# Two of four weight sums of a pair made by adding transfers on GpSimd's queue, with the weight slots turned and the normalisation and splits re-ordered to suit

## The chip, the cores and the metric

The kernel runs on one core of one Trainium2 chip. The metric is the device time of one execution in microseconds; times given are medians of several executions.

## The reference

One layer is computed: an RMS norm, a projection into eight attention heads and a pooling mixer, and an output projection with a second RMS norm and a residual. With a sequence of 512 and a width of 2048:

```python
hn = _rmsnorm(h, pre_norm_gain[layer])
proj = jnp.einsum('bsd,de->bse', hn, w_in[layer])        # 2048 -> 6 * 1024
q, k, v, g_a, u_b, g_b = jnp.split(proj, split_at, axis=-1)
y_a = _stick_breaking(heads(q), heads(k), heads(v))       # 8 heads of 128
y_a = y_a.transpose(0, 2, 1, 3).reshape(b, s, D_SB) * jax.nn.silu(g_a)
y_b = _multiscale_pool(u_b, w_pool[layer], pool_scale[layer]) * jax.nn.silu(g_b)
mix = jnp.concatenate([y_a, y_b], axis=-1)
out = jnp.einsum('bse,ed->bsd', mix, w_out[layer])
h = h + _rmsnorm(out, post_norm_gain[layer])
```

All of it is float32.

## The kernel before, in words

**Split operands.** TensorE multiplies in a rounded format, so each float32 operand is split in two: ScalarE copies it to a rounded high part (`w_hi`, `x_hi`, `a_hi`), VectorE subtracts to get the rest (`raw_lo`, `x_lo`, `a_lo`), and three matmuls (`three`, L1232 to L1234) make one product. `raw_lo` lies on the same bytes as `raw`, so a slot of `raw` is taken from the landing of its weights until the TensorE step that uses it is done. There are 7 such slots of 512 KB.

**Stage 1, the values.** `values_step(i)`, 16 steps, multiplies raw tokens times gain (`xT`, tiles of `mix`) by the value weights. In the same time the kernel prepares the left operands of everything that follows. ScalarE squares the token rows (`square_of`, L471, 128x2048 each), VectorE makes the mean square (`ms_col`), GpSimd raises it to -0.5 (L1205), and its queue stores this to DRAM (`rstd_dram`) and loads it back spread over all partitions (`rstd_rows`). `hn_of(q)` then normalises four tiles of `mix` in place (L847), and for each of four groups q seven operands of a Strassen product are made and split: A11, R1, S2, S4, S3, A12, A22. These have the counters `a_summed`, `a_hi_done` and `a_split`. Group q is spread over the iterations i = 4 + 3q, 5 + 3q and 6 + 3q of the loops of ScalarE and VectorE. In iteration i these engines also split x of step i + 3 and the weights of step i + 2. `v_drain` copies the finished values out of PSUM, scaled by `rstd_col`.

**Stage 2, the pairs (the body).** 20 units u of 7 products each (Strassen-Winograd: 7 products of 128x1024 weights in place of 8). Product p of unit u is `step_of(u, p)`, 24 matmuls. Its weights are four parts of two chunks (p = 0, 4, 3, 5, loaded by `load_b`) and four sums of them (p = 1, 2, 6, 4), made by VectorE in `w_sum` (L827). Between the products lie the score, suffix-sum, value and pooling matmuls of the heads; GpSimd masks (`mask`, L1216). The order of the work is written out by hand per unit kind r and product p. `ROLE[u][p]` is the slot of a product's weights: a permutation carried from unit to unit.

**Stage 3, the output projection.** `rows_tile` multiplies the split `mix` (`mix_hi_of`, `mix_lo_of` at L1032) by the split output weights (`o_hi_of` at L655, `o_lo_of` at L1041); squares, norm, residual and store follow.

**Queues.** All loads are on SyncE's queue. A load waits there for the step that frees its slot: before, (0, 4, 3, 5) of the next unit wait for steps 0, 1, 2, 3 of this one.

Of the kernel before, what the change touches and what calls it, by code (L numbers as in the profile page):

```python
# [5 lines left out]
F32 = mybir.dt.float32  # L6
# [77 lines left out]
def slot_turns():  # L84
# [10 lines left out]
    for u in range(UNITS):  # L95
        for p in (0, 4, 3, 5):
            lands((u, p), ROLE[u][p])
# [8 lines left out]
def hybrid_layer(nc, xT, x, pre_gain, w_v, w_heads, w_pool, pool_scale, w_out, post_gain, out):  # L106
    with ExitStack() as ctx:
# [27 lines left out]
        rstd_col = sb("rstd_col", [P, TT])  # L135
        ss_col = sb("ss_col", [P, TT])
# [88 lines left out]
        w_summed = sem("w_summed")  # L225
        step_done = sem("step_done")
# [6 lines left out]
        rstd_spread = sem("rstd_spread")  # L233
        hn_done = sem("hn_done")
# [108 lines left out]
        def _(sp):  # L343
# [26 lines left out]
            load_x_rows(0)  # L370
            load_x(4)
            load_v(4)
            load_x_rows(1)
            load_x_rows(2)
            load_x(5)
            load_v(5)
            load_x_rows(3)
            load_x(6)
            load_v(6)
            sp.dma_start(pool_scale_col[:, :], pool_scale).then_inc(scale_loaded, 16)  # L380
            for i in range(7, V_STEPS):
                load_x(i)
                load_v(i)
                if i == 15:
                    pass

            def load_b(u, p):
                n1, n2 = unit_chunks(u)
                n = n1 if p in (0, 5) else n2
# [8 lines left out]
            for p, last in ((0, 9), (4, 10), (3, 11), (5, 12)):  # L398
                sp.wait_ge(step_done, last + 1)
                load_b(0, p)  # L400
            for u in range(LAST_UNIT):
# [4 lines left out]
                for p, freed in ((0, 0), (4, 1), (3, 2), (5, 3)):  # L406
                    sp.wait_ge(step_done, step_of(u, freed) + 1)
                    if r == 3 and p == 5:
# [33 lines left out]
        def _(act):  # L442
# [11 lines left out]
            def w_hi_of(g):  # L454
# [5 lines left out]
                elif p in (0, 3, 5):  # L460
                    act.wait_ge(raw_loaded[slot], TURN[u, p])
                else:
                    act.wait_ge(w_summed, 4 * u + (1, 2, 6, 4).index(p) + 1)
# [22 lines left out]
            def a_hi_raw(q):  # L486
                act.wait_ge(hn_done, 4 * (q + 1))
                for op, half, tok in ((A11, 0, 0), (A12, 1, 0), (A22, 1, 1)):
                    act.activation(split3(operand(a_hi, op, q)), pairs(mix, q, half, tok),  # L489
                                   ACT.Copy).then_inc(a_hi_done, 1)  # L490

            def a_hi_sum(q, op):
                act.wait_ge(a_summed, 4 * q + (R1, S2, S3, S4).index(op) + 1)
                dst = operand(a_hi, op, q)
                if op == R1:
                    act.activation(dst, sum1[:, :], ACT.Copy).then_inc(a_hi_done, 1)
                elif op == S2:
                    act.activation(dst, sum2[:, :], ACT.Copy).then_inc(a_hi_done, 1)
                elif op == S3:
                    act.activation(split3(dst), pairs(mix, q, 0, 1), ACT.Copy).then_inc(a_hi_done, 1)  # L500
                else:
                    act.activation(split3(dst), pairs(mix, q, 1, 0), ACT.Copy).then_inc(a_hi_done, 1)
# [19 lines left out]
            x_hi_of(1)  # L522
            w_hi_of(1)
            x_hi_of(2)
            for i in range(V_STEPS):
                if i + 3 < V_STEPS:
                    x_hi_of(i + 3)
                w_hi_of(i + 2)
                if i == 1:
                    square_of(0)  # L530
                if i == 2:
                    square_of(1)
                    square_of(2)
                if i == 3:
                    square_of(3)
                q, part = (i - 4) // 3, (i - 4) % 3
                if i >= 4:
                    if part == 0:
                        a_hi_raw(q)
                        a_hi_sum(q, R1)  # L540
                    if part == 1:
                        a_hi_sum(q, S2)
                        a_hi_sum(q, S3)
                    if part == 2:
                        a_hi_sum(q, S4)
            act.wait_ge(rstd_ready, 1)
            v_drain(0, 0)
            v_drain(0, 1)
# [921 lines left out]
```

## Time and profile before

| what | value |
|---|---|
| median of 3 runs | 778.89 us (775.41 to 779.28) |
| the profiled execution | 779.01 us, span 777.3 us |
| mean granted TensorE clock | 0.98 |
| TensorE busy | 740.6 us of the span (95%) |
| VectorE, ScalarE busy | 525.5 us (68%), 389.8 us (50%) |
| stages | values to about 113 us, body from 119 to 584 us, output to the end |

The span runs from the first to the last instruction; the profiled execution took 1.7 us more than that. Busy shares are means over three stages that differ, so the stages are read apart. The granted clock is full at 1.00; 0.50 is the lower level.

### The profile page before, as it was taken

How to read it: one execution, taken by the hardware profiler on the slowest of the kernel's cores; microseconds unless marked ns; L12 is line 12 of the kernel's file. 1: busy time of each engine (PE TensorE's matmuls, PEld its weight loads, DVE VectorE, ACT ScalarE, POOL GpSimd, SP SyncE). 2: the span in 40 equal slices, each digit the busy share in tenths (PEclk: the TensorE clock that was granted, in tenths of full speed). 3: DMA queues.
4: the chain of work that ended last, by engine and by line, in shares of the span. 5: the costliest groups of instructions: out<-in, count | busy, mean ns of one | idle time of the engine just before them, and what ended most of it. 6: DMA issues, size and time to landing. Idle time of an engine off the chain costs nothing.

```text
span 777.3 us, 11793 instructions
## 1 busy us (share of the span) xinstructions
PE 740.6 (95%) x4912; PEld 685.2 (88%) x4912; DVE 525.5 (68%) x612; ACT 389.8 (50%) x530; POOL 29.8 (4%) x47
## 2 busy tenths in 40 slices
PE   7938988999999999999999999999997999999996
PEld 5827868999999999999999999999996888888885
DVE  4318896797977897877897977897867713142233
ACT  4615546655566655566655566655577522132200
POOL 0100000010000010010010010010000000000000
PEclk9977998999999999999999999999999999999999
DMA  8942203222233222233222233212245504142232
GB/s 322 381 108 63 87 28 108 82 74 98 91 109 109 79 73 98 92 110 109 78 72 98 94 109 109 77 71 98 96 147 206 183 35 162 55 149 78 99 136 108
DMA packets 27716, 87.02 MB, mean 112 GB/s; under 512 B 3152, under 2 KB 4176, under 8 KB 27024
## 3 DMA queue, kind: packets, MB, share of 16 engines
q1 hardware_dynamic: 27408, 86.00, 31.7%
q8 instruction: 39, 0.64, 0.3%
q0 software_dynamic: 112, 0.26, 0.2%
q14 instruction: 13, 0.11, 0.0%
q10 hardware_dynamic: 144, 0.01, 0.0%
HBM read 82.06 MB, written 4.20 MB: 111 GB/s over the span
## 4 chain that ended last, share of the span: by engine, by line
PE 83%; DVE 8%; ACT 3%; DMA 3%; issue 2%; POOL 0%; DVEq 0%; POOLq 0%; SPq 0%; ACTq 0%
PE ps L1232 27%; PE ps L1233 26%; PE ps L1234 26%; DVE raw_lo L802 2%; PE ps L1323 1%; PE ps L1321 1%; DVE mix L847 1%; DMA rstd_dram<-rstd_col 1%; DMA rstd_rows<-rstd_dram 1%; DVE a_lo L862 1%; ACT w_hi L466 1%; ACT a_hi L489 1%; PE ps L1249 0%; DVE a_lo L879 0%; DMA raw<-w_v 0%
## 5 line engine op out<-in xcount | busy, mean ns | idle before, releaser
L1232 PE MATMUL ps<-a_hi,w_hi 128*128 128x256 f32 x1120 | 319.8, 286 | 5.9 <-ACT mix L513 5.9
L1233 PE MATMUL ps<-a_lo,w_hi 128*128 128x256 f32 x1120 | 318.6, 284 | 0.0
L1234 PE MATMUL ps<-a_hi,raw_lo 128*128 128x256 f32 x1120 | 318.6, 284 | 0.0
L1232 PEld LDWEIGHTS ps<-a_hi,w_hi 128*128 128x128 f32 x1120 | 215.6, 192 | 6.6 <-issue 6.3
L1233 PEld LDWEIGHTS ps<-a_lo,w_hi 128*128 128x128 f32 x1120 | 215.5, 192 | 0.3
L1234 PEld LDWEIGHTS ps<-a_hi,raw_lo 128*128 128x128 f32 x1120 | 215.4, 192 | 0.0
L802 DVE TENSOR_TENSOR raw_lo<-raw,w_hi 128x1024 fp32r<-128x1024 f32 x155 | 189.6, 1223 | 37.9 <-ACT w_hi L466 37.3
L466 ACT ACTIVATE w_hi<-raw 128x1024 fp32r<-128x1024 f32 x155 | 163.5, 1055 | 75.2 <-PE ps L1234 73.0
L827 DVE TENSOR_TENSOR raw<-raw 128x1024 f32<-128x1024 f32 x80 | 98.7, 1234 | 1.5 <-PE ps L1234 1.5
L1232 PE MATMUL ps<-a_hi 128*128 128x512 f32 x192 | 75.5, 393 | 3.9 <-DVE a_lo L1032 3.9
L1234 PE MATMUL ps<-a_hi,a_lo 128*128 128x512 f32 x192 | 75.5, 393 | 0.0
L1233 PE MATMUL ps<-a_lo,a_hi 128*128 128x512 f32 x192 | 75.4, 393 | 0.0
L1232 PE MATMUL ps<-w_hi,x_hi 128*128 128x512 f32 x120 | 48.4, 403 | 14.4 <-DVE raw_lo L802 14.4
L1041 DVE TENSOR_TENSOR a_lo<-raw,a_hi 128x1024 fp32r<-128x1024 f32 x24 | 28.3, 1222 | 42.3 <-ACT a_hi L655 42.3
L1233 PE MATMUL ps<-raw_lo,x_hi 128*128 128x512 f32 x120 | 48.5, 404 | 0.0
L1234 PE MATMUL ps<-w_hi,x_lo 128*128 128x512 f32 x120 | 48.4, 404 | 0.0
L1232 PEld LDWEIGHTS ps<-a_hi 128*128 128x128 f32 x192 | 36.3, 189 | 11.8 <-issue 4.1
L655 ACT ACTIVATE a_hi<-raw 128x1024 fp32r<-128x1024 f32 x24 | 24.0, 1049 | 44.6 <-PE ps L1234 44.6
L1216 POOL TENSOR_SCALAR_AFFINE_SELECT tri<-tri 128x256 f32<-128x256 f32 x32 | 24.1, 775 | 527.4 <-DVE tri L951 429.0
L1234 PEld LDWEIGHTS ps<-a_hi,a_lo 128*128 128x128 f32 x192 | 36.4, 189 | 7.6
L1233 PEld LDWEIGHTS ps<-a_lo,a_hi 128*128 128x128 f32 x192 | 36.3, 189 | 7.6
L1232 PEld LDWEIGHTS ps<-w_hi,x_hi 128*128 128x128 f32 x120 | 23.3, 194 | 20.2 <-issue 14.8
(140 smaller groups left out, 849.4 us busy)
## 6 DMA issues: line engine op xcount, KB each, us to landing
raw<-w_heads SPq DMA_DIRECT2D x80, 512.0 KB, 3.5
raw<-w_out SPq DMA_DIRECT2D x32, 512.0 KB, 4.8
raw<-w_v SPq DMA_DIRECT2D x15, 512.0 KB, 10.0
mix<-xT SPq DMA_DIRECT2D x16, 256.0 KB, 9.9
x_rows<-x SPq DMA_DIRECT2D x4, 1024.0 KB, 13.6
raw<-x SPq DMA_DIRECT2D x8, 512.0 KB, 4.4
out<-mix SPq DMA_DIRECT2D x6, 512.0 KB, 2.7
wp_raw<-w_pool SPq DMA_DIRECT2D x8, 128.0 KB, 2.1
```

The source lines that it names most:

```text
L466: act.activation(hi_slot(g), raw_slot(raw, slot), ACT.Copy).then_inc(w_hi_done, 1)
L489: act.activation(split3(operand(a_hi, op, q)), pairs(mix, q, half, tok), ACT.Copy).then_inc(a_hi_done, 1)
L655: act.activation(out_weights(a_hi, o_hi3, n % OUT_SLOTS)[:, b * QUARTER:(b + 1) * QUARTER], raw_slot(raw, half_slot(j)), ACT.Copy).then_in ...
L802: dve.tensor_tensor(raw_slot(raw_lo, slot), raw_slot(raw, slot), hi_slot(g).bitcast(F32), ALU.subtract).then_inc(w_split, 1)
L827: dve.tensor_tensor(raw_slot(raw, ROLE[u][p]), raw_slot(raw, ROLE[u][a]), raw_slot(raw, ROLE[u][b]), ALU.add).then_inc(w_summed, 1)
L847: dve.scalar_tensor_tensor(mix_tile(k), mix_tile(k), pre_gain_col[:, k:k + 1], rstd_rows[:, :], ALU.mult, ALU.mult).then_inc(hn_done, 1)
L862: dve.tensor_tensor(split3(operand(a_lo, op, q)), pairs(mix, q, half, tok), split3(operand(a_hi, op, q)).bitcast(F32), ALU.subtract).then_ ...
L1041: dve.tensor_tensor(out_weights(a_lo, o_lo3, n % OUT_SLOTS)[:, cols], raw_slot(raw, half_slot(j)), out_weights(a_hi, o_hi3, n % OUT_SLOTS) ...
L1216: pool.affine_select(out=sq, in_=sq, compare_op=ALU.is_gt, fill=0.0, base=0, pattern=[[0, 2], [1, P]], channel_multiplier=-1).then_inc(don ...
L1232: pe.matmul(dst, sta[0], mov[0], start=first, stop=False, skip_group_check=True)
L1233: pe.matmul(dst, sta[0], mov[1], start=False, stop=False, skip_group_check=True)
L1234: return pe.matmul(dst, sta[1], mov[0], start=False, stop=last, skip_group_check=True)
```

## The change

Five edits come together.

1. `t1` (p = 1, was 0 + 4) and `t3` (p = 4, was a part of its own with 4 + 3) are no longer VectorE sums. SyncE loads one part plainly into the slot of p = 1 and of p = 4; GpSimd's queue then issues a transfer of 512 KB that adds the other part to it in SBUF (`add_b`). In this split of the work p = 1 takes the first part of both chunks, and p = 4 the two second parts. VectorE keeps p = 2 and p = 6. ScalarE waits for the new counters `t1_summed` and `t3_summed`.
2. `ROLE` and the order of loads follow: five plain loads per unit, (1, 0, 4, 3, 5), waiting for steps 0 to 4.
3. The token rows are loaded earlier, in a layout with four consecutive tokens on a partition; the squares follow at once; the reciprocal root is stored and spread by ScalarE's queue, the store in runs of 16 bytes. A third small transfer brings `rstd_col`.
4. The order of splitting the operands is turned to A11, R1, S2, S4, S3, A12, A22, the order of the products, and S3, A12, A22 of the last group are split in the first products of the body. The first product waits for A11 alone.
5. In the last unit the splits of `mix` tiles 0 to 3 come at products 1 to 3, and the first output weights are split ahead of the softplus.

```diff
-ROLE = [[2, 6, 0, 4, 3, 5, 1]]
+ROLE = [[3, 2, 0, 5, 4, 6, 1]]
-    ROLE.append([_r[0], _r[4], _r[5], _r[2], _r[1], _r[3], _r[6]])
+    ROLE.append([_r[1], _r[0], _r[5], _r[3], _r[2], _r[4], _r[6]])
...
+            by_four = x.rearrange("t (q s) d -> (t q) s d", s=TT)
-                sp.dma_start(x_rows[:, s * D:(s + 1) * D], x[s]).then_inc(x_rows_loaded[s], 16)
+                sp.dma_start(x_rows[:, s * D:(s + 1) * D], by_four[:, s, :]).then_inc(x_rows_loaded[s], 16)
...
-            for p, last in ((0, 9), (4, 10), (3, 11), (5, 12)):
+            for p, last in ((1, 9), (0, 10), (4, 11), (3, 12), (5, 13)):
...
-                for p, freed in ((0, 0), (4, 1), (3, 2), (5, 3)):
+                for p, freed in ((1, 0), (0, 1), (4, 2), (3, 3), (5, 4)):
...
+                elif p == 1:
+                    act.wait_ge(t1_summed, 16 * (u + 1))
+                elif p == 4:
+                    act.wait_ge(t3_summed, 16 * (u + 1))
...
+                if i == 3:
+                    act.wait_ge(rstd_ready, 1)
+                    act.dma_start(rstd_dram.rearrange("(p s) -> p s", s=TT),
+                                  rstd_by_four[:, :]).then_inc(rstd_sent, 16)
...
+                if i == 3:
+                    act.wait_ge(rstd_sent, 16)
+                    act.dma_start(rstd_rows[:, :],
+                                  rstd_dram.partition_broadcast(P)).then_inc(rstd_spread, 16)
+                    act.dma_start(rstd_col[:, :], rstd_dram.rearrange("(s p) -> p s", p=P),
+                                  allow_slow_non_contiguous=True).then_inc(rstd_col_loaded, 16)
...
                     if last:
                         if p == 1:
                             mix_hi_of(0)
-                        if p == 4:
-                            for k in (1, 2, 3):
-                                mix_hi_of(k)
-                        if p == 5:
-                            o_hi_of(0)
+                            mix_hi_of(1)
+                        if p == 2:
+                            mix_hi_of(2)
+                            mix_hi_of(3)
...
+            def a_sum4(q):
+                dve.wait_ge(a_split, PRODUCTS * q + R1 + 1)
+                dve.wait_ge(a_summed, 4 * q + 2)
+                dve.scalar_tensor_tensor(split3(sum1[:, :]), pairs(mix, q, 1, 0), -1.0,
...
-                    if p == 1:
-                        w_sum(u, 4)
-                    if p in (5, 6) and not last:
-                        w_sum(u + 1, p - 4)
+                    if p == 6 and not last:
+                        w_sum(u + 1, 2)
+                    if u == 0 and p < 3:
+                        a_lo_of(3, (S3, A12, A22)[p])
...
+            def add_b(u, p, done):
+                slot = ROLE[u][p]
+                a = 0 if p == 1 else QUARTER
+                pool.wait_ge(raw_loaded[slot], TURN[u, p])
+                if u:
+                    pool.wait_ge(w_hi_done, step_of(u - 1, p) + 1)
+                pool.dma_start(raw_slot(raw, slot), w_heads[unit_chunks(u)[1]][:, a:a + QUARTER],
+                               accum_op=ALU.add).then_inc(done, 16)
+            add_b(0, 1, t1_summed)
+            add_b(0, 4, t3_summed)
+            for u in range(UNITS):
...
+                if r in (0, 2) and u:
+                    h = h0 - 1 if r == 0 else h0
+                    pool.wait_ge(weights_exp, h + 1)
+                    mask(weights_masked)
+                if u < LAST_UNIT:
+                    add_b(u + 1, 1, t1_summed)
+                if r in (1, 4):
+                    pool.wait_ge(softplus_done, h0 + 1 if r == 1 else h0 + 2)
+                    mask(softplus_masked)
+                if u < LAST_UNIT:
+                    add_b(u + 1, 4, t3_summed)
...
-                    pe.wait_ge(a_split, PRODUCTS * 3 + (1, 4, 5, 7, 7, 7, 7)[p])
+                    pe.wait_ge(a_split, PRODUCTS * 3 + p + 1)
```

ScalarE in the values stage, the kernel before, from the split of x of step 4 on (L451 splits x, L466 the weights, L471 squares token rows, L489 is the first operand copy):

```order
L451 ACTIVATE x_hi0<-mix,pre_gain_col 128x512 [waits step_done,x_loaded4]
L466 ACTIVATE w_hi<-raw 128x1024 [waits step_done,raw_loaded3]
L471 ACTIVATE x_rows,ss_col<-x_rows 128x2048 [waits x_rows_loaded0]
L451 ACTIVATE x_hi1<-mix,pre_gain_col 128x512 [waits step_done,x_loaded5]
L466 ACTIVATE w_hi<-raw 128x1024 [waits step_done,raw_loaded4]
L471 ACTIVATE x_rows,ss_col<-x_rows 128x2048 [waits x_rows_loaded1]
L471 ACTIVATE x_rows,ss_col<-x_rows 128x2048 [waits x_rows_loaded2]
L451 ACTIVATE x_hi2<-mix,pre_gain_col 128x512 [waits step_done,x_loaded6]
L466 ACTIVATE w_hi<-raw 128x1024 [waits step_done,raw_loaded5]
L471 ACTIVATE x_rows,ss_col<-x_rows 128x2048 [waits x_rows_loaded3]
```

The same place now (L470 splits weights, L475 squares):

```order
L475 ACTIVATE x_rows,ss_col<-x_rows 128x2048 [waits x_rows_loaded2]
L475 ACTIVATE x_rows,ss_col<-x_rows 128x2048 [waits x_rows_loaded3]
L451 ACTIVATE x_hi0<-mix,pre_gain_col 128x512 [waits step_done,x_loaded4]
L470 ACTIVATE w_hi<-raw 128x1024 [waits step_done,raw_loaded4]
L451 ACTIVATE x_hi1<-mix,pre_gain_col 128x512 [waits step_done,x_loaded5]
L533 DMA rstd_dram<-rstd_by_four 128x4 [waits rstd_ready]
L451 ACTIVATE x_hi2<-mix,pre_gain_col 128x512 [waits step_done,x_loaded6]
L470 ACTIVATE w_hi<-raw 128x1024 [waits step_done,raw_loaded5]
L541 DMA rstd_rows<-rstd_dram 128x512 [waits rstd_sent]
L543 DMA rstd_col<-rstd_dram 128x4x1
L451 ACTIVATE x_hi3<-mix,pre_gain_col 128x512 [waits step_done,x_loaded7]
L470 ACTIVATE w_hi<-raw 128x1024 [waits step_done,raw_loaded6]
```

All four squares now stand ahead of the split of step 4, and ScalarE's own queue waits for the store to land before it goes on to x of step 7 and the weights of step 6.

GpSimd, from the reciprocal root into the first units, before:

```order
L1205 TENSOR_TENSOR rstd_col<-ms_col,neg_half 128x4 [waits vec_const,ms_ready]
L1208 DMA rstd_dram<-rstd_col 128x4x1 [waits rstd_ready]
L1211 DMA rstd_rows<-rstd_dram 128x512 [waits rstd_sent]
L1216 AFFINE_SELECT tri<-tri 128x2x128 [waits softplus_done]
L1216 AFFINE_SELECT tri<-tri 128x256
```

and now (L1228 is the adding transfer, L1218 the mask):

```order
L1212 TENSOR_TENSOR rstd_by_four<-ms_col,neg_half 128x4 [waits vec_const,ms_ready]
L1228 DMA raw<-w_heads 128x1024 [waits raw_loaded2]
L1228 DMA raw<-w_heads 128x1024 [waits raw_loaded4]
L1228 DMA raw<-w_heads 128x1024 [waits w_hi_done,raw_loaded3]
L1228 DMA raw<-w_heads 128x1024 [waits w_hi_done,raw_loaded0]
L1228 DMA raw<-w_heads 128x1024 [waits w_hi_done,raw_loaded2]
L1218 AFFINE_SELECT tri<-tri 128x2x128 [waits softplus_done]
L1218 AFFINE_SELECT tri<-tri 128x256
```

Forty adding transfers stand between the sixteen pairs of masks, two for each unit.

ScalarE at the end of the last unit, before (L643 splits `mix` tiles, L590 the softplus, L655 output weights):

```order
L466 ACTIVATE w_hi<-raw 128x1024 [waits step_done,w_summed]
L643 ACTIVATE a_hi<-mix 128x512 [waits y_free,step_done] x3
L590 ACTIVATE tri_hi<-tri 128x1280 [waits pool_done,softplus_masked]
L655 ACTIVATE a_hi<-raw 128x1024 [waits raw_loaded2,step_done]
L655 ACTIVATE a_hi<-raw 128x1024 [waits raw_loaded3]
```

and now (L470, L665 and L600 are the same operations):

```order
L470 ACTIVATE w_hi<-raw 128x1024 [waits step_done,w_summed]
L665 ACTIVATE a_hi<-raw 128x1024 [waits raw_loaded2,step_done]
L665 ACTIVATE a_hi<-raw 128x1024 [waits raw_loaded3]
L600 ACTIVATE tri_hi<-tri 128x1280 [waits pool_done,softplus_masked]
```

The three `mix` tiles have gone to earlier products, and the output weights no longer stand behind the masked softplus.

## Rows read from the trace of the kernel before

**Rows 1.** The page, part 1: busy us, share of the span, instructions.

```profile
PE 740.6 (95%) x4912; PEld 685.2 (88%) x4912; DVE 525.5 (68%) x612; ACT 389.8 (50%) x530; POOL 29.8 (4%) x47
```

**Rows 2.** Waits of TensorE: us in total, times, longest.

```profile
PE ps L1232 <- DVE raw_lo L802: 14.4, 1, 14.4
...
PE ps L1232 <- DVE a_lo L1032: 3.9, 1, 3.9
```

**Rows 3.** Timeline of TensorE: start us, us, instruction, idle time before it.

```profile
12.64 0.40 PE L1232 MATMUL ps<-w_hi,x_hi 128*128 128x512 f32 x1
...
46.01 0.39 PE L1234 MATMUL ps<-w_hi,x_lo 128*128 128x512 f32 x1
60.80 0.76 PE L1232 MATMUL ps<-w_hi,x_hi 128*128 128x512 f32 x1 [14.40 <-DVE raw_lo L802]
...
67.17 0.39 PE L1232 MATMUL ps<-w_hi,x_hi 128*128 128x512 f32 x1
...
112.94 0.40 PE L1234 MATMUL ps<-w_hi,x_lo 128*128 128x512 f32 x1
...
119.20 0.55 PE L1232 MATMUL ps<-a_hi,w_hi 128*128 128x256 f32 x1 [5.87 <-ACT mix L513]
...
125.05 0.28 PE L1232 MATMUL ps<-a_hi,w_hi 128*128 128x256 f32 x1
...
588.03 0.48 PE L1232 MATMUL ps<-a_hi 128*128 128x512 f32 x1 [3.91 <-DVE a_lo L1032]
```

**Rows 4.** TensorE by stretch: length, busy (matmuls), granted clock, DMA share, GB/s.

```profile
64.00:66.00 2.00, 2.00 (x6) 0.50 0.00 0
...
122.00:125.00 3.00, 3.00 (x16) 0.50 0.00 0
...
590.00:592.00 2.00, 2.00 (x6) 0.50 1.02 354
```

**Rows 5.** The chain that ended last, 0 to 180 us: start, us, what.

```profile
31.34 2.00 ACT x_rows L471 x2
...
34.93 10.12 DMA rstd_dram<-rstd_col
...
45.35 7.50 DMA rstd_rows<-rstd_dram
```

**Rows 6.** Timeline of ScalarE, the split of x of step 5.

```profile
24.41 0.72 ACT L451 ACTIVATE x_hi<-mix,pre_gain_col 128x512 fp32r<-128x512 f32 x1 [3.37 <-DMA mix<-xT]
```

**Rows 7.** DMA issues: count, KB each, median us from issue to landing.

```profile
raw<-w_heads SPq DMA_DIRECT2D x80, 512.0 KB, 3.5
...
rstd_rows<-rstd_dram POOLq DMA_DIRECT2D x1, 256.0 KB, 7.5
pre_gain_col<-pre_gain ACTq DMA_DIRECT2D x1, 8.0 KB, 3.0
```

**Rows 8.** Timeline of VectorE in the values stage, groups 1 to 3.

```profile
70.19 2.73 DVE L847 SCALAR_TENSOR_TENSOR mix<-mix,pre_gain_col,rstd_rows 128x512 f32<-128x512 f32 x4
...
75.79 0.75 DVE L794 SCALAR_TENSOR_TENSOR x_lo<-mix,pre_gain_col,x_hi 128x512 fp32r<-128x512 f32 x1 [2.15 <-ACT x_hi L451]
...
104.16 2.74 DVE L847 SCALAR_TENSOR_TENSOR mix<-mix,pre_gain_col,rstd_rows 128x512 f32<-128x512 f32 x4
```

**Rows 9.** All engines by stretch, the body (PE, PEld, DVE, ACT, POOL busy).

```profile
130.00:580.00 450.00, 450.00 (x3630) 445.37 (x3629) 369.81 (x407) 271.91 (x359) 23.35 (x30) 1.00 0.27 96
```

**Rows 10.** Timeline of ScalarE in one unit (r = 3).

```profile
308.64 0.38 ACT L557 ACTIVATE q_raw<-ps 128x256 f32<-128x256 f32 x1 [1.55 <-PE ps L1234]
...
324.48 1.06 ACT L466 ACTIVATE w_hi<-raw 128x1024 fp32r<-128x1024 f32 x1 [0.78 <-PE ps L1234]
...
330.18 0.39 ACT L557 ACTIVATE mix<-ps 128x256 f32<-128x256 f32 x1 [1.03 <-PE ps L1234]
```

**Rows 11.** Timelines at the end of the last unit: ScalarE, then VectorE.

```profile
579.77 1.27 ACT L590 ACTIVATE tri_hi<-tri 128x1280 fp32r<-128x1280 f32 x1 [2.95 <-POOL tri L1216]
...
582.03 2.36 DVE L1041 TENSOR_TENSOR a_lo<-raw,a_hi 128x1024 fp32r<-128x1024 f32 x2 [2.58 <-ACT a_hi L655]
```

More of the change, by code:

```diff
@@ L95, in slot_turns @@
     for u in range(UNITS):
-        for p in (0, 4, 3, 5):
+        for p in (1, 0, 4, 3, 5):
             lands((u, p), ROLE[u][p])
@@ L369, in _ @@
                 load_v(i)
[L370 to L376, printed above, removed]
+                load_x_rows(i - 1)
             load_x_rows(3)
-            load_x(6)
-            load_v(6)
+            for i in (4, 5, 6):
+                load_x(i)
+                load_v(i)
             sp.dma_start(pool_scale_col[:, :], pool_scale).then_inc(scale_loaded, 16)
@@ L726, in _ @@
                         if p == 5:
+                            if last:
+                                o_hi_of(0)
                             softplus_hi_of(h1)
@@ L859, in a_lo_raw @@
                 dve.tensor_tensor(a21, pairs(mix, q, 0, 0), a21, ALU.subtract).then_inc(a_summed, 1)
-                for n, (op, half, tok) in enumerate(((A11, 0, 0), (A12, 1, 0), (A22, 1, 1))):
-                    dve.wait_ge(a_hi_done, PRODUCTS * q + n + 1)
-                    dve.tensor_tensor(split3(operand(a_lo, op, q)), pairs(mix, q, half, tok),
-                                      split3(operand(a_hi, op, q)).bitcast(F32),
-                                      ALU.subtract).then_inc(a_split, 1)
@@ new lines, in a_lo_of @@
+            def a_lo_of(q, op):
+                dve.wait_ge(a_hi_done, PRODUCTS * q + op + 1)
+                hi, lo = operand(a_hi, op, q).bitcast(F32), operand(a_lo, op, q)
+                if op in (A11, A12, A22, S3):
+                    half, tok = {A11: (0, 0), A12: (1, 0), A22: (1, 1), S3: (0, 1)}[op]
+                    dve.tensor_tensor(split3(lo), pairs(mix, q, half, tok), split3(hi),
+                                      ALU.subtract).then_inc(a_split, 1)
+                else:
+                    dve.tensor_tensor(lo, (sum2 if op == S2 else sum1)[:, :], hi,
@@ L915, in _ @@
                         hn_of(q)
+                        a_lo_of(q, A11)
                     if part == 1:
-                        a_lo_raw(q)
+                        a_sums(q)
+                        a_lo_of(q, R1)
+                        a_lo_of(q, S2)
                     if part == 2:
-                        a_lo_sums(q)
+                        a_sum4(q)
+                        a_lo_of(q, S4)
+                        if i < V_STEPS - 1:
+                            for op in (S3, A12, A22):
+                                a_lo_of(q, op)
             def combine(u, p):
```

170 lines of the change are left out of this document (71 added, 99 removed).

## The prediction

> **What bounds the kernel now.** I read the shares first: TensorE is busy for 740.6 of 777.3 us [rows 1], so at most 36.7 us of the span can be won without fewer matmuls. Then its waits, which say where these lie. Three stand after the start: 14.4 us for the low part of a weight (VectorE), 5.9 us for a drain of the values (ScalarE), and 3.9 us for a split `mix` tile (VectorE) [rows 2, 3]. Then the body alone: from 130 to 580 us TensorE is busy for 450.00 of 450.00 us at full clock, VectorE for 369.81 and ScalarE for 271.91 [rows 9]. So in the body nothing waits for VectorE, and work taken from VectorE there gives nothing by itself. The reader should see that the change is worth what it does to the two ends of the body, less what its new waits cost inside.
>
> Each gap costs more than its length. After the 14.4 us gap the stretch 64 to 66 us has a granted clock of 0.50, after the 5.9 us gap the stretch 122 to 125 us has it too, and after the 3.9 us gap 590 to 592 us [rows 4]: 1.2 in place of 2.4 GHz, after TensorE had stood still.
>
> The chain tells why the first gap is there. The last square ends at 33.3, the store of the root begins 1.6 us later and takes 10.12 us, the spread 7.50 us, to 52.9 [rows 5]; VectorE, whose order has `hn_of(0)` ahead of the weights of step 7, stands until then, and TensorE, done with step 6 at 46.2, until 60.8 [rows 3].
>
> **Term 1, the values stage.** Steps 1 to 6 ran from 12.64 to 46.24 (46.01 plus one pitch of 0.23), 5.60 us each; later, at full clock, 201 matmuls went from 67.17 to 113.17, a pitch of 0.229 or 5.49 us for a step of 24 [rows 3]. With no wait the stage ends at 12.64 + 6 x 5.60 + 9 x 5.49 = 95.7 us, and the first product starts there, not at 119.2: 23.5 us.
>
> Does it have no wait? (a) The rows. x of step 5 landed at 24.4 [rows 6], behind 7,168 KB in queue order. That is now the place of the last token rows: the last square runs from 24.4 to 26.4, and the root is ready 1.6 us later as before, at 28.0. x and weights of step 4 are 768 KB more; at the mean rate so far (7,168 KB in 24.4 us) that is 2.6 us, so they are there at 27.0, and copy (1.0) and subtraction (1.2) end at 29.2. Step 4 starts at 12.64 + 3 x 5.60 = 29.4. That just fits; half a microsecond lost is possible. (b) The round trip. ScalarE issues the store after the splits of steps 4 and 5, at about 28.7. A store on its queue: the nearest row is the gain's load, 128 rows on the same queue, 3.0 us [rows 7]; the other end is 10.1 us, the old store [rows 5], which had four times as many pieces. I take 3.5. The spread: the old one took 7.5 on GpSimd's queue [rows 5]; the lower end is 3.0, the gain's row. I take 5.0, between. Behind the wait for the store stand x of step 7 and the weights of step 6 (wanted at 40.6), behind the spread `hn_of(0)` and then the weights of step 7 (wanted at 46.2). After the rows land, VectorE and ScalarE need some 6.8 us: normalising 2.7 [rows 8], ScalarE's copies of A11, R1 and x 0.6 to 0.7 each, copy and subtraction of the weights 2.2. Landing by 39.4 costs nothing. 28.7 + 3.5 + 0.4 + 5.0 = 37.6: no wait. Store and spread together may take 10.3 us. (c) The pace. A group of three iterations took (104.16 - 70.19) / 2 = 17.0 us on VectorE, of which 2.15 us was a wait for x_hi behind four operand copies of ScalarE [rows 8]. Now two copies stand ahead of it and one split (0.6 us) lies in the wait: about 1 us of wait left, and 0.7 more for S4: some 16.5 us, against 16.5 that TensorE needs for three steps. It keeps pace. (d) The end. The drain waited for S4, the last sum (ScalarE, before); now it stands ahead of S4, and product 0 wants A11 only. The 5.9 us go; they are within the 23.5.
>
> **Term 2, clock at the start of the body.** From 119.20 to 125.05 the matmuls had a pitch of 0.213; at full clock it is 0.12. 27 matmuls x 0.094 = 2.6 us. Without the gap this is not paid.
>
> **Term 3, the end of the last unit.** VectorE waited 2.58 us for the split of the first output weights, which ScalarE made behind the masked softplus (579.77) [rows 11]; the `mix` tiles followed, and TensorE stood 3.9 us [rows 2]. TensorE had ended product 6 at 588.03 - 3.91 = 584.1 [rows 3]; product 4 was done two products of 2.9 us and 1.4 us of pooling earlier, at about 577. Now the weights are split from then on, 2 us on ScalarE and 1.2 more on VectorE, which is through by 582, and the tiles were made earlier. I take the whole 3.9 and, for 8 matmuls at half the clock [rows 4], pitch 0.43 instead of 0.23, 1.6, less 0.5 for a remainder: 5.0 us.
>
> **Term 4, the body.** VectorE loses 40 sums, SyncE gains 20 loads, GpSimd gains 40 adding transfers. The load of p = 1 of the next unit is issued when product 0 is done (308.64), lands 3.5 us later (312.1) [rows 7, 10]; then the adding transfer starts. ScalarE took up these weights at 324.48, and TensorE wanted them at about 330.1, when product 0 of the next unit was done [rows 10]; copy and subtraction take 2.3 us, so the transfer may take 330.1 - 2.3 - 312.1 = 15.7 us at no cost. For p = 4 the room is no smaller: its load comes two products later and its use three. In units where a mask stands ahead in GpSimd's queue, the mask waits for matmuls that lengthen the unit as much. What does an adding transfer of 512 KB take? No row shows one. Lower end: 3.5 us, the plain load [rows 7]. Upper end: the 256 KB spread on the same software queue, 7.5 us, doubled: 15.0. Being on that queue and reading two streams, I take 10. All three are under 15.7, so the term is 0, hidden behind five products.
>
> The Trainium skill ("DMA: Bandwidth & Descriptors", Anatomy of one DMA) gives 2.0 us plus bytes over 436 GB/s for a transfer of GpSimd's queue. By it 512 KB take 3.2 us and the 256 KB spread 2.6, where the trace has 7.5; the trace decides, and by the page term 4 is 0 as well, with a wider margin.
>
> **Sum.** 779.0 - 23.5 - 2.6 - 5.0 - 0 = 747.9, say 748.0 us. It is made against the profiled execution (779.01), which stands 0.1 us above the median of the runs.
>
> **Rivals.**
> - *The round trip of the root stays slow.* For it: the loads of the values stage still fill the same transfer engines then, and the old store took 10.1 us. With 5.0 and 7.5 us the rows land at 41.6, 2.2 us late: 750 us. With the old 10.1 and 7.5 the rows land at 46.7, and step 7 starts 7.3 us late; the half clock after it took 15 matmuls from 60.80 to 67.17 [rows 3], 15 x (0.425 - 0.229) = 2.9 us: 758.2. Against: a quarter of the pieces, another queue. Chance 0.20.
> - *The hand-over still waits.* ScalarE's drain, or the low parts that follow it, come late in the first unit, as before: 5.9 + 2.6 stay: 756.5. Against: a drain now needs only the first 0.7 us of step 15 and A-operands of groups done long ago. Chance 0.07.
> - *Slower: the adding transfers land too late.* If one takes X us, each of the 19 units that follow another pays X - 15.7, ScalarE's queue standing at the copy of p = 1 and VectorE behind it. The gain of 31.1 is eaten at X = 15.7 + 31.1 / 19 = 17.3. The mechanism that could bring it there: GpSimd writes the pieces of each transfer itself beside a VectorE that is busy for 82% of the body [rows 9]. If it had only VectorE's idle 18% for that, each microsecond of writing would take 5.6: 15.0 + 4.6 = 19.6 for one such microsecond, and 748 + 19 x 3.9 = 822 us. The Trainium skill ("SBUF — State Buffer", Who interferes with whom) says that VectorE's two-port modes lock GpSimd out of writing descriptors, but that tensor_tensor, the form here, is inferred not to. Chance 0.08.
> - *The adds are late in some kinds of unit only,* by 1 to 2 us: 755 to 768. Chance 0.05.
> - *The forecast:* 745 to 750.5. Chance 0.60.
>
> **How the numbers follow.** About 0.5% (4 us) is what a measurement of this kernel can tell from no change. All cases but the third end below 775: faster 0.90, same 0.02 (adds late by 1.5 us), slower 0.08. The range takes in the forecast, the slow round trip and the late hand-over, and about 1 us for the runs' own spread: 744 to 760.
>
> **What would show it.** In the profile after: the first body matmul near 96 us; no TensorE wait over 1 us between 12 and 560; granted clock 1.00 throughout; `hn_of(0)` starting near 38; the first `rows_tile` right behind product 6. The landing time of the adding transfers decides term 4: under 15.7 us it is nothing, and ScalarE's copies of p = 1 stand where they stood. Wrong would be: a wait of TensorE for ScalarE's or VectorE's weights once per unit, or a body longer than 465 - 2.6 us.

## The result and the profile after

The changed kernel takes **754.49 us** (median of 4 runs, 753.12 to 756.16), the kernel before on the same chip 779.09 us (775.41 to 780.76): ratio **0.9691, 95% interval 0.9652 to 0.9731**. The profiled execution took 756.16 us with a span of 754.4; it is the longest of the four.

The page of the changed kernel first, busy time of each engine and, of the 40 slices, TensorE and its granted clock:

```profile
PE 736.1 (98%) x4912; PEld 679.6 (90%) x4912; DVE 481.5 (64%) x572; ACT 389.9 (52%) x530; POOL 62.4 (8%) x85
...
PE   7999989999999999999999999999999999999996
...
PEclk9999999999999999999999999999999999999999
```

TensorE has the same 4,912 matmuls as in [rows 1]; its 4.5 us less of busy time are matmuls that no longer run at half clock. The prediction took the 36.7 us of idle time as the most that can be won without fewer matmuls; that is too little by this part, since matmuls at half clock count as busy. VectorE has 40 instructions and 44 us less, and GpSimd twice its busy time. What won the time is in TensorE's waits (engine, tile, line, releaser: us in total, times, longest), where 14.4, 5.9 and 3.9 us stood before [rows 2, 3]:

```profile
PE ps L1274 <- ACT w_hi L520: 5.3, 1, 5.3
...
PE ps L1257 <- DVE raw_lo L813: 2.4, 2, 1.8
PE ps L1257 <- ACT p_neg L571: 1.3, 1, 1.3
PE ps L1257 <- ACT mix L514: 1.1, 1, 1.1
PE ps L1257 <- ACT work L567: 1.1, 1, 1.1
```

The first is the start of the program and was there before. TensorE's timeline has the places of the others, and the first `rows_tile` matmul, which now has no gap ahead of it:

```profile
49.71 0.47 PE L1257 MATMUL ps<-w_hi,x_hi 128*128 128x512 f32 x1 [1.84 <-DVE raw_lo L813]
...
101.45 0.36 PE L1257 MATMUL ps<-a_hi,w_hi 128*128 128x256 f32 x1 [1.11 <-ACT mix L514]
...
108.53 0.36 PE L1257 MATMUL ps<-a_hi,w_hi 128*128 128x256 f32 x1 [1.09 <-ACT work L567]
...
112.97 0.36 PE L1257 MATMUL ps<-a_hi,w_hi 128*128 128x256 f32 x1 [1.33 <-ACT p_neg L571]
...
566.88 0.40 PE L1257 MATMUL ps<-a_hi 128*128 128x512 f32 x1
```

With 119.20 and 588.03 from [rows 3] these split the 22.9 us between the spans (the medians of the runs are 24.6 us apart, as the profiled execution of the changed kernel is its longest):

| stretch | before | after | difference | predicted |
|---|---|---|---|---|
| to the first product of the body | 119.20 | 101.45 | -17.75 | -23.5 |
| the body, to the end of product 6 | 464.92 | 465.43 | +0.5 | -2.6 |
| from there to the end, gap included | 193.18 | 187.52 | -5.66 | -5.0 |

The first row hangs on the pair of executions. Two runs below have the values stage of the kernel before, but for a sum or two on VectorE; their first product starts at 122.01 and 121.52. Six have the one of the changed kernel, and start it at 99.05 to 101.85. The means (120.9 of three, 100.4 of seven) are 20.5 us apart, not 17.75.

The stretches behind the two hand-overs, and the body (length; PE, PEld, DVE, ACT, POOL busy; granted clock, DMA share, GB/s), answer to [rows 4, 9]:

```profile
102.00:105.00 3.00, 3.00 (x28) 3.00 (x26) 2.30 (x4) 1.18 (x3) 0.00 (x0) 1.00 0.00 0
...
567.00:569.00 2.00, 2.00 (x11) 1.62 (x10) 1.44 (x2) 1.97 (x4) 0.00 (x0) 1.00 0.61 154
...
130.00:560.00 430.00, 430.00 (x3465) 425.31 (x3464) 313.58 (x355) 262.47 (x346) 50.75 (x64) 1.00 0.61 161
```

The clock is full in all three. In the body TensorE is again busy all the time, while VectorE's busy share falls from 82% to 73%: nothing waited for it, so nothing came of that. The DMA issues (KB each, median us to landing) have the adding transfers, and the round trip of the root:

```profile
raw<-w_heads SPq DMA_DIRECT2D x100, 512.0 KB, 4.2
raw<-w_heads POOLq DMA_DIRECT2D x40, 512.0 KB, 6.4
...
rstd_rows<-rstd_dram ACTq DMA_DIRECT2D x1, 256.0 KB, 6.7
rstd_dram<-rstd_by_four ACTq DMA_DIRECT2D x1, 2.0 KB, 6.0
```

ScalarE's timeline in the values stage shows how that trip lies: store issued at 29.84, spread at 35.84, and x of step 7 behind the wait for the store. In the chain, VectorE's first group (`mix` L848) starts at 42.61, the next at 59.34 and 76.07:

```profile
29.84 0.33 ACTq L533 DMA_DIRECT2D rstd_dram<-rstd_by_four  x1
...
35.84 0.33 ACTq L541 DMA_DIRECT2D rstd_rows<-rstd_dram  x1
...
37.03 0.72 ACT L451 ACTIVATE x_hi<-mix,pre_gain_col 128x512 fp32r<-128x512 f32 x1 [3.66 <-PE ps L1259]
```

```profile
29.84 5.97 DMA rstd_dram<-rstd_by_four
35.84 6.75 DMA rstd_rows<-rstd_dram
42.61 2.75 DVE mix L848 x4
...
59.34 2.75 DVE mix L848 x4
...
76.07 2.74 DVE mix L848 x4
```

### The profile page after: what moved, and what is told of

Its sections match the earlier page's. It is cut to its first block, busy times and chain, and to the rows that moved or that the text cites. A ratio compares the mean times of both kernels' runs of the same rounds, so it can differ in the third digit from the quotient of the medians.

```text
span 754.4 us, 11839 instructions
## 1 busy us (share of the span) xinstructions
PE 736.1 (98%) x4912; PEld 679.6 (90%) x4912; DVE 481.5 (64%) x572; ACT 389.9 (52%) x530; POOL 62.4 (8%) x85
## 4 chain that ended last, share of the span: by engine, by line
PE 83%; DVE 7%; DMA 4%; issue 3%; ACT 2%; SPq 1%; DVEq 0%; POOLq 0%; POOL 0%; ACTq 0%
PE ps L1257 27%; PE ps L1258 27%; PE ps L1259 27%; DMA mix<-xT 2%; PE ps L1348 1%; DVE mix L848 1%; DVE raw_lo L813 1%; PE ps L1346 1%; DMA rstd_rows<-rstd_dram 1%; DVE a_lo L881 1%; DVE a_lo L878 1%; DMA rstd_dram<-rstd_by_four 1%; ACT w_hi L470 1%; SPq L367 1%; DVE sum L853 0%
## 5 line engine op out<-in xcount | busy, mean ns | idle before, releaser
L813 DVE TENSOR_TENSOR raw_lo<-raw,w_hi 128x1024 fp32r<-128x1024 f32 x155 | 189.3, 1223 | 58.7 <-ACT w_hi L470 58.0
L470 ACT ACTIVATE w_hi<-raw 128x1024 fp32r<-128x1024 f32 x155 | 163.5, 1055 | 75.7 <-PE ps L1259 71.5
L1228 POOL DMA_DIRECT2D raw<-w_heads x40 | 34.9, 871 | 322.4 <-DMA raw<-w_heads 286.1
L828 DVE TENSOR_TENSOR raw<-raw 128x1024 f32<-128x1024 f32 x40 | 48.8, 1220 | 10.5 <-DMA raw<-w_heads 9.5
L665 ACT ACTIVATE a_hi<-raw 128x1024 fp32r<-128x1024 f32 x24 | 24.1, 1051 | 45.2 <-PE ps L1259 45.2
L1218 POOL TENSOR_SCALAR_AFFINE_SELECT tri<-tri 128x256 f32<-128x256 f32 x32 | 24.0, 772 | 165.3 <-ACT tri L604 84.9
```

The costliest lines, as they stand in the source:

```text
L470: act.activation(hi_slot(g), raw_slot(raw, slot), ACT.Copy).then_inc(w_hi_done, 1)
L665: act.activation(out_weights(a_hi, o_hi3, n % OUT_SLOTS)[:, b * QUARTER:(b + 1) * QUARTER], raw_slot(raw, half_slot(j)), ACT.Copy).then_in ...
L813: dve.tensor_tensor(raw_slot(raw_lo, slot), raw_slot(raw, slot), hi_slot(g).bitcast(F32), ALU.subtract).then_inc(w_split, 1)
L828: dve.tensor_tensor(raw_slot(raw, ROLE[u][p]), raw_slot(raw, ROLE[u][a]), raw_slot(raw, ROLE[u][b]), ALU.add).then_inc(w_summed, 1)
L1218: pool.affine_select(out=sq, in_=sq, compare_op=ALU.is_gt, fill=0.0, base=0, pattern=[[0, 2], [1, P]], channel_multiplier=-1).then_inc(don ...
L1228: pool.dma_start(raw_slot(raw, slot), w_heads[unit_chunks(u)[1]][:, a:a + QUARTER], accum_op=ALU.add).then_inc(done, 16)
```

## The experiments

Four questions: which part of the change wins the time; why the first term came 5.75 us short; how much room the adding transfers have; what the better order would give.

### Which part wins

**The changed kernel without adding transfers.** The values stage and the end as changed; in the body the old sums, slots and loads.

```diff
+                    if p == 1:
+                        w_sum(u, 4)
-                    if p == 6 and not last:
-                        w_sum(u + 1, 2)
+                    if p in (5, 6) and not last:
+                        w_sum(u + 1, p - 4)
...
-            add_b(0, 1, t1_summed)
-            add_b(0, 4, t3_summed)
```

> The changed kernel with the four sums back on VectorE, the old slots and the four plain loads; the new values stage and the new end are kept. Theory A (the adding transfers are hidden and the sums on VectorE were never waited for in the body; the gain is at the two ends): 754 to 758 us, the only cost being one or two sums of 1.2 us on VectorE at the hand-over to the body. Theory B (the adding transfers cost time in the body, by their load on DMA or by late landing): 3 us or more under the changed kernel, 751 us or less. Theory C (the sums taken from VectorE are the gain): 770 us or more.

Measured 755.72 us (755.11 to 758.16), ratio 0.9703 (0.9675 to 0.9731): the changed kernel's time.

**The adding transfers alone,** put into the kernel before with their slots and loads.

> The kernel before with the adding transfers, their slots and loads, and nothing else of the change. Theory A: 776 to 779 us, since the body has no wait to win and only the hand-over has one or two sums less. Theory B: over 779. Theory C: 755 to 765 us.

Measured 780.14 us (777.30 to 781.75), ratio 1.0005 (0.9989 to 1.0021). The time is above the 776 to 779 us expected, but the kernel before took 780.00 us beside it. With the run above this settles it from both sides: the transfers neither win nor cost anything that can be measured.

**The end's order,** undone in the changed kernel, and alone in the kernel before; VectorE's part moves with ScalarE's, whose lines these are.

```diff
...
                         if p == 1:
                             mix_hi_of(0)
-                            mix_hi_of(1)
-                        if p == 2:
-                            mix_hi_of(2)
-                            mix_hi_of(3)
+                        if p == 4:
+                            for k in (1, 2, 3):
+                                mix_hi_of(k)
+                        if p == 5:
+                            o_hi_of(0)
...
```

> The changed kernel with the old order of splits in the last unit. By my term 3, with its size from the traces (3.9 us wait and 1.7 us of half clock): 754.5 + 5.6 = 760 us, with the wait of 3.9 us back. Rival (the end is bound by the landing of the output weights or by the masked softplus in any order, and the wait went because the sums left VectorE): 754 to 756 us.

> The kernel before with only the new order of the last unit's end. Theory A (the 3.9 us wait goes, and some 1.7 us behind it): 774 to 775 us. Rival (it needs the new values stage or the adding transfers' room): 779 to 780 us, or only the 3.9 us of the wait, 776 us.

Undone: 760.82 us (760.05 to 762.36), ratio 0.9764 (0.9734 to 0.9795), with the wait of 3.90 us for a `mix` split back. Alone: 774.28 us (771.89 to 775.88), ratio 0.9936 (0.9910 to 0.9962). By the ratios the end is worth 5.7 us in the one company and 5.0 in the other, so it doesn't depend on the rest. That leaves some 19 us, all from the values stage.

### Why the first term came short

**Rows of roots from other data, loaded at the start.** Tokens aren't normalised by their own root; store and spread stay, but `hn_of(0)` doesn't wait for them.

> The changed kernel, but rstd_rows is filled at the start with other data (a part of the output gain), so that nothing waits for the spread of the root; the tokens are thus not normalised by their own root, everything else is computed. Theory A (the 6 us by which the gain fell short are the slow round trip: the 1.8 us wait at step 7 and the lag of VectorE that it leaves, paid again as 1.1 + 1.1 + 1.3 us at the hand-over): all of it goes, about 749 us, first body matmul near 97.5. Rival (the waits at the hand-over come from the order of ScalarE and VectorE there and not from a lag): only the 1.8 us go, 752.7 us, and the three waits of about 1 us stay.

Measured 752.48 us (752.17 to 752.62), ratio 0.9655 (0.9633 to 0.9678). The first product starts at 98.08; the gap at step 7 and the one at the hand-over are gone. Two waits in the first unit, 0.84 and 1.35 us, stand as before. So the late rows cost 2 to 3 us (3.4 us between the two profiled starts, 2.3 us against the mean of 100.4), and the first unit's waits are another thing; the forecast of 749 was wrong in taking all for one. The rival's 752.7 us is the time measured, though the wait at the hand-over, which it kept, went.

**The old round trip in the changed kernel:** store by single elements and spread on GpSimd's queue, old layout.

```diff
-                sp.dma_start(x_rows[:, s * D:(s + 1) * D], by_four[:, s, :]).then_inc(x_rows_loaded[s], 16)
+                sp.dma_start(x_rows[:, s * D:(s + 1) * D], x[s]).then_inc(x_rows_loaded[s], 16)
...
+            pool.dma_start(rstd_dram.rearrange("(s p) -> p s", p=P), rstd_col[:, :],
+                           allow_slow_non_contiguous=True).then_inc(rstd_sent, 16)
+            pool.wait_ge(rstd_sent, 16)
+            pool.dma_start(rstd_rows[:, :], rstd_dram.partition_broadcast(P)).then_inc(rstd_spread, 16)
```

> The changed kernel with the round trip of the roots as before: the store by single 4-byte elements, the spreading transfer on GpSimd's queue, the old layout of the rows. Theory A (what the new values stage wins rests on the quick store): store about 10 and spread about 7.5 us put the rows of roots at about 47 instead of 42.5 us; the wait at the sixth step grows from 1.8 to some 6 us, the clock may fall to 0.50 behind it: 760 to 766 us. Rival (the order of the steps alone does it and the trip lies beside them): 754 to 756 us.

Measured 762.38 us (760.19 to 762.86), ratio 0.9762 (0.9743 to 0.9781). Its chain has the two transfers, its timeline of TensorE the wait, and the stretch behind it the clock:

```profile
29.05 13.90 DMA rstd_dram<-rstd_col
43.26 5.54 DMA rstd_rows<-rstd_dram
```

```profile
55.91 0.77 PE L1252 MATMUL ps<-w_hi,x_hi 128*128 128x512 f32 x1 [8.20 <-DVE raw_lo L803]
```

```profile
56.00:58.00 2.00, 2.00 (x5) 1.61 (x6) 2.00 (x4) 1.60 (x3) 0.00 (x0) 0.50 0.00 0
```

The trip takes 19.4 us in place of 12.7, the wait grows by 6.4 us, and the kernel loses 5.5 us by the ratios, 7.9 by the medians. So of the 19 us that the values stage wins some 7 are the quicker store. Whether its runs of 16 bytes or its other queue make it quicker isn't shown, since the run changes both; the spread was no slower on GpSimd's queue (5.54 us against 6.75). The rest falls to the earlier token rows and the order; no run takes these two apart.

**The first unit's drains one product later.** ScalarE took two drains of the values stage ahead of the copy that frees a PSUM tile for TensorE; the second pair waited 1.95 us for VectorE:

```profile
106.87 1.24 ACT L514 ACTIVATE mix<-ps,rstd_col 128x512 f32<-128x512 f32 x2
108.01 0.37 ACT L567 ACTIVATE work<-ps 128x256 f32<-128x256 f32 x1
...
111.28 1.26 ACT L514 ACTIVATE mix<-ps,rstd_col 128x512 f32<-128x512 f32 x2 [1.95 <-DVE a_lo L878]
112.44 0.38 ACT L571 ACTIVATE p_neg<-ps 128x256 f32<-128x256 f32 x1
```

```diff
-                    if u == 0 and p < 3:
-                        for s in ((2, 3), (0, 1), (2, 3))[p]:
-                            v_drain(int(p > 0), s)
+                    if u == 0 and p in (1, 2, 3):
+                        for s in ((2, 3), (0, 1), (2, 3))[p - 1]:
+                            v_drain(int(p > 1), s)
```

> The changed kernel with only the first unit's drains of the values stage moved one product later, behind the first unit's copies. Theory A (the waits of 1.09 and 1.33 us in the first unit come from ScalarE taking two drains ahead of a copy that TensorE waits for): these two go, the 1.84 us at the sixth step and the 1.11 us at the hand-over stay: 752 us. Rival (they follow from the late rows of roots): no change, 754.5 us.

Measured 753.13 us (753.07 to 755.00), ratio 0.9669 (0.9637 to 0.9702). Both waits are gone from the profile (one of 0.85 us for a weight's low part is new); the time moved by 1.4 us, which the interval alone wouldn't tell from nothing.

**Both places.** As well as the drains, the first group's normalising, A11 and R1 come one step later, behind the weights of step 7.

```diff
-                    if part == 0:
+                    if part == 0 and q > 0:
...
+                        if q == 0:
+                            hn_of(q)
+                            a_lo_of(q, A11)
```

> The changed kernel with two places of its order moved: the first group's VectorE work that needs the rows of roots comes one step later in the values stage, and the first unit's drains of the values stage come one product later, behind the first unit's copies. Nothing is left out. Theory A (the misses of the first term are order, not hardware: waits of 1.84, 1.11, 1.09 and 1.33 us): most of these 5.4 us go, about 750 us. Rival (what is moved is only late elsewhere: ScalarE or VectorE is the limit of this stretch): 753 to 757 us, with the same waits at other products.

Measured **751.06 us** (750.52 to 751.63), ratio **0.9623 (0.9608 to 0.9637)**, an interval below the changed kernel's. All four waits are gone; there are 1.44 us at an early step (32.50, ahead of both places moved) and 0.16 in the first unit instead. The lost time was order, not the speed of an engine: behind the places moved nothing over 0.16 us turned up. The same with VectorE's sums in place of the adding transfers:

> The kernel with both places of the order moved (751.1 us) and the weight sums on VectorE in place of the adding transfers. Theory A (in the body VectorE isn't waited for, so its sums cost nothing): 750 to 753 us. Rival (with the other waits gone VectorE's 49 us more of work show): 755 us or more.

Measured 749.75 us (749.65 to 750.64), ratio 0.9623 (0.9592 to 0.9653): again no difference. TensorE's waits, after the start, are a single one:

```profile
PE ps L1265 <- ACT w_hi L516: 5.8, 1, 5.8
PE ps L1248 <- DVE raw_lo L812: 0.7, 1, 0.7
```

### How much room the adding transfers have

**Held back to step 4 and to step 5 of the unit before.** The adding transfer for p = 1 goes out then, and the one for p = 4 right behind it (0.9 us later).

```diff
-                    pool.wait_ge(w_hi_done, step_of(u - 1, p) + 1)
+                    pool.wait_ge(step_done, step_of(u - 1, 4 if p == 1 else 3) + 1)
```

> The changed kernel, but each adding transfer of the pair's second weight sum goes out only once step 4 of the unit before is done (the other sum's after step 3); nothing is left out. Theory A (the adding transfers cost nothing because they land well ahead of need: they took 6.4 us, and ScalarE needs their result by about 327.8 us in a unit whose step 4 ends at 321.6): the result comes at 328.0, so 0 to 0.3 us a unit, in all 0 to 6 us over the changed kernel: 754 to 761 us. Theory B (the room is smaller than I worked out, say ScalarE wants its input two or three us earlier): 2 to 3 us in each of some 19 units, 790 to 815 us.

> As the run that waits for step 4, but the wait is for step 5, 2.9 us later in each unit. Theory A (room ends where I worked out): the result is 3.1 us late in each of some 19 units: 754 + 59 = about 813 us, with a TensorE wait of about 3 us a unit; more if such gaps lower the granted clock to 0.50. Theory C (VectorE and ScalarE have slack that takes the delay up, or the transfer lands sooner than 6.4 us when it runs alone): under 790 us, with waits under 1.5 us.

Measured 810.74 us (807.85 to 816.76), ratio 1.0391 (1.0332 to 1.0450), and 840.61 us (837.66 to 841.78), ratio 1.0764 (1.0739 to 1.0789). The first is far off what I expected by my own theory. In the timelines of the run with step 4, GpSimd issues at 304.38, and ScalarE, free since 305.5, gets the sum at 311.89:

```profile
304.38 1.79 POOL L1228 DMA_DIRECT2D raw<-w_heads  x2 [11.58 <-PE ps L1259]
```

```profile
311.89 1.06 ACT L470 ACTIVATE w_hi<-raw 128x1024 fp32r<-128x1024 f32 x1 [6.38 <-DMA raw<-w_heads]
```

7.5 us, where the changed kernel's median was 6.4. Over the six transfers between 275 and 405 us the times are 6.0 to 7.7, mean 7.3. With step 5 it is 5.4 to 5.9, mean 5.5, as here from 317.07 to 322.58:

```profile
317.07 1.78 POOL L1228 DMA_DIRECT2D raw<-w_heads  x2 [14.32 <-PE ps L1259]
```

```profile
322.58 1.06 ACT L470 ACTIVATE w_hi<-raw 128x1024 fp32r<-128x1024 f32 x1 [7.25 <-DMA raw<-w_heads]
```

**The second transfer apart.** The first waits for step 4, the second for step 5, so that the first has no other adding transfer behind it.

> As the run whose first adding transfer waits for step 4, but the second one waits for step 5, so that the first goes alone. In the run before, the first sum reached ScalarE 6.0 to 7.7 us after its issue. Theory A (the second adding transfer, issued 0.9 us behind it, lengthens it from some 5.5 to 7.5 us): it lands some 2 us sooner, the waits of 1.9 us a unit go, 755 to 765 us. Theory B (SyncE's own loads, or the place in the unit, set the time: with step 5 both adding transfers went together too, and the first took only 5.4 to 5.9 us): 800 to 812 us as before.

Measured 808.27 us (802.07 to 813.84), ratio 1.0395 (1.0330 to 1.0460); the first one takes 6.4 to 7.8 us, mean 7.3, as before. So the second isn't what lengthens it. What the two runs with step 4 share is SyncE's plain load of another part, which step 4 releases too, with the pooling weights behind it, 0.5 us ahead of the adding transfer (302.13):

```profile
301.62 0.33 SPq L392 DMA_DIRECT2D raw<-w_heads  x1
301.99 0.43 SPq L396 DMA_DIRECT2D wp_raw<-w_pool  x1
```

In the run with step 5 no other queue moved a byte in the stretch from 317.1 to 322.6, and it moved 121 GB/s; the run with step 4 moved 198 from 304.4 to 311.9. That the load is the cause fits all three runs, but no run took it away. The two stretches differ in VectorE too, busy for 1.65 us in the run with step 4 and for none in the one with step 5. GpSimd's own time for issuing two transfers was the same in both, 1.79 and 1.78 us.

**The room, measured.** By my working ScalarE can wait until 6.2 us after the end of step 4: 327.8 against 321.6, where ScalarE's copy in the kernel before waits for that step.

```profile
321.60 1.06 ACT L466 ACTIVATE w_hi<-raw 128x1024 fp32r<-128x1024 f32 x1 [1.82 <-PE ps L1234]
```

The means put the sums at 7.3 and 2.9 + 5.5 = 8.4 us after it, 1.1 and 2.2 us late. TensorE's waits are 38.4 us with step 4:

```profile
PE ps L1257 <- DVE raw_lo L813: 15.5, 9, 2.0
PE ps L1257 <- ACT mix L575: 12.6, 4, 3.5
PE ps L1346 <- DVE tri_lo L966: 11.0, 6, 2.7
```

(less 0.7 in the values stage), and by the same three lines 58.7 us with step 5: 2.0 and 3.1 us as a mean over 19 units. Both are 0.9 us more than my working gives. So a transfer may take 14.8 us at no cost, not 15.7. One thing that the working left out is in the lines: it followed the weights alone, but ScalarE also has drains behind that copy. In the unit above the copy of the sum ended at 312.95, three gate instructions followed, and TensorE stood for the drain behind them:

```profile
314.71 0.36 ACT L575 ACTIVATE mix<-ps 128x256 f32<-128x256 f32 x1
```

```profile
315.21 0.55 PE L1257 MATMUL ps<-a_hi,w_hi 128*128 128x256 f32 x1 [2.75 <-ACT mix L575]
```

The four waits of this kind have a mean of 3.2 us, the others 1.8. The rest of the loss is the clock. A mean of 0.974, against 0.998 in the changed kernel, is 2 x 0.024 x 811 = 39 us more at half clock, which cost some 19.5 (an estimate): 38.4 + 19.5 = 57.9 for the 56.8 us between the spans. With step 5 the same working gives 58.7 + 21 for 81.5 us.

## Why the prediction was right, and where it wasn't

It forecast 748.0 us, in a range of 744 to 760, and 754.5 came. The forecast's own band, 745 to 750.5, was missed; faster was right. That 754.5 lies in the range is owed to the room left for two rivals, not to the sum. Of the signs named, the last one was met: a body longer than 462.4 us was to be wrong, and it took 465.4. It wasn't the adding transfers, though, but two waits in the first unit. By its steps:

- **Term 4, the body: right, at 0.** The adding transfers took 6.4 us, between the ends of 3.5 and 15.0; I had taken 10. The room was 14.8 us by experiment, 15.7 by my working. The argument that VectorE isn't waited for, so that its 40 sums buy nothing, is shown from both sides (755.72 without the transfers, 780.14 with them alone). The slower rival had the right form for a cost (each of 19 units pays what exceeds the room, as the delayed runs do) and the wrong size: the transfers would have to take over twice as long. Its mechanism, GpSimd slowed beside a busy VectorE, doesn't show: the 40 issues took 0.86 to 1.06 us each, with VectorE busy for 73% of the body. Beside it, the clock makes such waits dearer than I priced them, by half again in the run with step 4. By the formula of the Trainium skill ("DMA: Bandwidth & Descriptors", Anatomy of one DMA) 512 KB take 3.2 us, an estimate; in this case's traces the adding form took 5.4 to 5.9 us with no other queue at work.
- **Term 3, the end: right.** 5.0 forecast, 5.66 in the table, 5 to 6 in two experiments.
- **Term 2, the clock behind the hand-over: right.** The stretch 102 to 105 us has 1.00 though a wait of 1.11 us stands ahead of it. It is in the body's row as -2.6.
- **Term 1, the values stage: right in kind, 5.75 us too large.** Three things in it. (b) was mis-sized: the store took 6.0 us, not 3.5, and the spread 6.7, not 5.0; issued at 29.84 and not 28.7, it put the rows at 42.6, where 39.4 was to cost nothing. I had interpolated towards an idle-queue load of 3.0 us, under loads that held the transfer engines. It cost 1.84 us at step 7; and (c) was too kind by a hair, since VectorE's groups came every 16.73 us against 3 x 24 x 0.2333 = 16.8 of TensorE, so the lag was never made up and came out as 1.11 us at the hand-over. (a) cost 0.59 us, as the text had allowed. (d) The drain no longer waits for S4, but the 5.9 us became 1.1. These waits are 3.5 of the 5.75 us. A further 1.0 is the pitch: 9 steps at 5.60 us and not 5.49. The last 1.2 us are in the timeline too: step 1 began at 13.25 and not 12.64, and each of the three gaps cost 0.2 us more than the idle time listed, which counts from the end of a matmul (0.39 us after its start) where the next would have started after 0.23.
  How much the late rows cost differs between profiled executions with the same values stage (in us: rows landed, wait at step 7, start of the first product):

  | execution | rows | wait | first product |
  |---|---|---|---|
  | changed kernel | 42.6 | 1.84 | 101.45 |
  | drains later | 41.4 | 1.09 | 100.31 |
  | old end | 41.6 | 1.00 | 100.49 |
  | held to step 4 | 41.3 | 0.69 | 100.13 |
  | the same, second apart | 40.5 | 0.34 | 99.34 |
  | no adding transfers | 40.1 | none | 99.05 |
  | held to step 5 (1.68 us lost ahead) | 43.0 | 0.47 | 101.85 |

  So the 1.84 us are the high end; the wait at the hand-over is 1.1 us in all but the one that didn't wait at step 7 (0.68). By the means of all executions with either stage the term is 20.5 us, 3.0 short of the 23.5.
- **The body's +0.5 in place of -2.6:** 2.42 us are the two waits of the first unit, which the prediction named only as part of the rival "hand-over still waits". That rival was partly right: neither 5.9 nor the clock, but the drains did come between. I had read ScalarE's queue for the first product alone and not for the second and third. Counted from start to start (107.16 to 108.53 and 111.36 to 112.97, at a pitch of 0.12) these two gaps cost 2.7 us, and 0.4 is left unexplained.
- **The rival "slow round trip"** is the one that came nearest: rows at 41.6 forecast there, 42.6 measured; 750 us forecast, and what the trip cost is 2 to 3 us. The 758.2 for the old trip is 762.4 in the experiment, since the old store took 13.9 us in this company, not 10.1, and the spread 5.5, not 7.5.

## What to carry to other kernels

Work taken from an engine that nobody waits for buys nothing; here 40 sums moved from VectorE to adding transfers are worth 0, while the earlier root and the order of a few splits and drains on two engines are worth 25 us, and 29 with two more places moved. A room worked out from one unit's timeline (issue, landing, last start that makes nobody wait) was good to 0.9 us in 15, so it is worth doing before moving a transfer; but take the transfer's time under the loads that run beside it, not from one that ran alone. And after a big wait is removed, read the queues of the two or three products behind the hand-over row by row: that is where the remainder sat.

## What the runs showed that I had not expected

- An adding transfer of 512 KB took 5.4 to 5.9 us issued at step 5, where the stretch looked at had no other queue at work, 6.4 in the median of the changed kernel (5.2 to 9.4), and 6.0 to 7.8 when they were issued at step 4, beside plain loads; plain loads took 3.5 (before) and 4.2 us (changed) in the median.
- A store of 2 KB took 6.0 us in runs of 16 bytes on ScalarE's queue (5.4 to 7.0 over the runs), and 10.1 [rows 5] to 13.9 us in single elements on GpSimd's, all under the loads of the values stage.
- Waits of 1.84 us and less left the granted clock at 1.00 (50 to 52 and 102 to 105 us). With the transfers held back to step 4, a wait of 2.33 us that ended at 285.82 was followed by 0.86 and then 0.50:

```profile
286.00:288.00 2.00, 2.00 (x12) 1.91 (x13) 2.00 (x3) 0.68 (x1) 0.00 (x0) 0.86 0.09 27
288.00:290.00 2.00, 2.00 (x11) 2.00 (x10) 2.00 (x3) 0.08 (x1) 0.00 (x0) 0.50 0.00 0
```

  The length of the wait alone doesn't decide it. In the same run a wait of 1.89 us that ended at 259.68 was followed by 0.53, and one of 2.04 us at 128.30 by 1.00; with the transfers held to step 5, one of 3.30 us at 378.83 was followed by 1.00:

```profile
260.00:262.00 2.00, 2.00 (x12) 2.00 (x11) 2.00 (x4) 1.70 (x3) 0.00 (x0) 0.53 0.28 109
```

```profile
130.00:132.00 2.00, 2.00 (x17) 1.87 (x16) 2.00 (x3) 0.84 (x3) 0.00 (x0) 1.00 0.04 8
```

```profile
382.00:386.00 4.00, 4.00 (x35) 4.00 (x35) 2.52 (x3) 2.67 (x4) 1.63 (x2) 1.00 0.06 16
```

- At one granted clock of 1.00 the 512-column matmuls of the values stage have a pitch of 0.2333 us in some stretches and 0.229 in others: the kernel before has the first until 46 us and the second behind its long gap, the adding transfers alone and the new end alone have 0.229 from the start, and the changed kernel and all its variants 0.2333 throughout. Nothing in the traces says why.
